# ACT copies the placed gates out ahead of the gelu of the same step, in the first part of the expert mixer

## The chip, the cores and the metric

The kernel runs on one core of one Trainium2 chip. The metric is the device time of one execution in microseconds (us); the time before is the median of three runs. Engines: PE (matrix multiply; PEld is its weight load), DVE (vector), ACT (scalar), POOL (GpSimd), SP (issues DMAs).

## The reference

One inference step of a two-layer backbone over 128 context tokens and 512 latent tokens of width 1024. Each layer is a token mixer (gated convolution with a recurrence in layer 0, attention in layer 1) and then an expert mixer, which the change touches. For the expert mixer each token has 8 heads; a head picks 16 of 128 x 128 experts by the sums of two score tables, and an expert is one row of `u_tab` and one row of `v_tab`:

```python
sc, pos = lax.top_k(cand, PEER_TOPK)
eidx = jnp.take_along_axis(cidx, pos, axis=-1)
gate = jax.nn.softmax(sc, axis=-1)
a = jax.nn.gelu(jnp.einsum('td,tkd->tk', xi, u_tab[ei]), approximate=False)
return jnp.einsum('tk,tkd->td', gi * a, v_tab[ei])
```

All is float32.

## The kernel before

The expert mixer is `peer`, called once per layer. It treats the five blocks of 128 tokens in two ways. Two blocks are *gathered*: POOL fetches each token's expert rows by indirect DMA, DVE multiplies a fetched row with the token (`meet`, L1610) and later adds a weighted row of `v` (`add_row`, L1628). The three others are *dense*: the products of all 384 tokens with all 16384 experts are computed, and the gates, which are zero but for 128 experts of a token, are laid out as a dense table in DRAM.

The dense blocks take two parts. The first has `STEPS` = 128 steps, one per tile of 128 experts. In step i

- DVE turns a tile of `u` (`turn`, L1601; it runs two steps ahead, with two buffers `u_turned` between it and PE),
- PE multiplies it with the tokens (`dots_of`, L1370, 8 products in 16 instructions) into one of four PSUM banks,
- ACT takes the gelu out of that bank (`gelu`, L1446) and sends it to DRAM (`store_acts`, L1451; two buffers `act_out`, so gelu i waits for the landing of store i - 2).

Beside this the dense gates are built. A group is 8 tokens; there are 16 groups in each of the stages 1, 2 and 3 of 32 steps (stage 0 is spent on choosing experts), in 26 steps of stages 1 and 2 and in 20 steps of stage 3 (`groups_at`). A group n passes through four engines' programs in successive steps:

1. step i, DVE: `one_hot(n)` writes two tables of ones and zeros (L1590, L1592);
2. step i + 1, ACT: `apply_gate(n)` scales one of them by the gates (L1465, 8 instructions);
3. step i + 2, PE: `place_gates(n)`, right behind that step's dots, multiplies the two tables (L1387, two halves of 8 instructions) into PSUM banks 6 and 7; half 0 waits until ACT has copied out half 0 of group n - 1, half 1 for half 1, and the whole for `apply_gate(n)`;
4. step i + 3, ACT: `gates_out(n)` copies both halves to `arena` (L1475, two instructions), and for an odd n sends 1 MB to DRAM (L1480, semaphore `gates_stored`).

The order on each engine is the order in which its block is written; engines meet only at semaphores. ACT's block is a loop over steps; in a step it takes the gelu, its store, at the start of a stage a softmax (`softmax`, L1440) and `choice_out` (L1458), then `gates_out`, `apply_gate`, and at the end `activate` (L1486, the gelu of eight gathered products). PE's block in a step is `dots_of`, `turn_choice` (L1377), `place_gates`. In the first three steps of stages 1 to 3 DVE also runs `decode` (L1549 to L1573), and in stages 0 to 2 it chooses experts for a later block (`choose`, L1521 to L1537), its first part in one step, its second in the next, none in the third. Both kinds of stores (L1451, L1480) are issued by ACT, on one queue; SP issues the loads of `u` (L1253).

The second part (L1417, L1628, L1635) multiplies the gated products with `v`; it isn't changed.

Of the kernel before, what the change touches and what calls it, by code (L numbers as in the profile page):

```python
# [1105 lines left out]
def groups_at(i):  # L1106

    stage, r = divmod(i, STAGE)
    first, steps = 16 * (stage - 1), 20 if stage == 3 else 26
    if i < 0 or not 1 <= stage <= 3 or not 5 <= r < 5 + steps:  # L1110
        return range(0)
    return range(first + 16 * (r - 5) // steps, first + 16 * (r - 4) // steps)
# [8 lines left out]
def decode_at(i):  # L1121

    stage, r = divmod(i, STAGE)
    return (stage - 1, r) if 1 <= stage <= 3 and r < 3 else None
# [26 lines left out]
def halves_by(i):  # L1151

    return range(picks_by(i - 1) // 8, picks_by(i) // 8)


def peer(nc, s, m, a, l):
# [88 lines left out]
    with phase(nc, f"q_full q_out s_full s_out keys_full keys_out w_landed*2 late_landed*2 u_landed*{U_SLOTS} u_ready dots_full "  # L1245
# [176 lines left out]
        @block.scalar  # L1422
        def _(act):
            def query_out(c, late):
                at = c + CHUNKS * late
                act.wait_ge(S.q_full, at + 1)
                if at >= 2:
                    act.wait_ge(S.s_full, at - 1)
                n = ND if late else N0
                nc.scalar.activation(q_cur[:, c % 2, 0:n], m.ps[:, c % 2, 0:n], ACT.Copy).then_inc(S.q_out, 1)  # L1430

            def scores_out(c, late):
                act.wait_ge(S.s_full, c + CHUNKS * late + 1)
                t0, t1 = (GATHERED, T) if late else (0, GATHERED)
                src = m.ps[:, 2 + c % 2, 0:(t1 - t0) * P].rearrange("p (t n) -> p t n", n=P)
                nc.scalar.activation(scores[:, t0:t1, c // 2, c % 2], src, ACT.Copy).then_inc(S.s_out, 1)

            def softmax(t):
                act.wait_ge(S.soft_ready, t + 1)
                nc.scalar.activation(gate, gate, ACT.Exp).then_inc(S.exp_ready, 1)  # L1440

            def gelu(i):
                act.wait_ge(S.dots_full, i + 1)
                if i >= ACT_SLOTS:
                    act.wait_ge(S.act_stored[i % ACT_SLOTS], 16 * (i // ACT_SLOTS))
                nc.scalar.activation(act_out[:, i % ACT_SLOTS], m.ps[:, i % 4, 0:ND], ACT.Gelu)\  # L1446
                    .then_inc(S.gelu_done, 1)

            def store_acts(i):
                act.wait_ge(S.gelu_done, i + 1)  # L1450
                act.dma_start(m.act_rows[i, :, 0:ND], act_out[:, i % ACT_SLOTS])\  # L1451
                    .then_inc(S.act_stored[i % ACT_SLOTS], 16)

            def choice_out(t):
                act.wait_ge(S.choice_full, t + 1)
                if t >= 1:
                    act.wait_ge(S.hot_ready, GROUPS * t)
                nc.scalar.activation(chosen, m.ps[:, 4, 0:3 * P].rearrange("p (s t) -> p s t", s=3), ACT.Copy)\  # L1458
                    .then_inc(S.choice_out, 1)

            def apply_gate(n):
                act.wait_ge(S.hot_ready, n + 1)
                for tok in range(HOT):
                    one, at = hot_i[:, n % 2, tok], n % GROUPS * HOT + tok
                    e = nc.scalar.activation(one, one, ACT.Copy, scale=chosen[:, 2, at:at + 1])  # L1465
                e.then_inc(S.gated, 1)

            def gates_out(n):
                g = n // 2
                for half in range(2):  # L1470
                    act.wait_ge(S.gates_full, 2 * n + half + 1)
                    if n % 2 == 0 and half == 0 and g >= 2:
                        act.wait_ge(S.gates_stored[g % 2], 16 * (g // 2))
                    at = n % 2 * HOT + half * 4
                    nc.scalar.activation(gates[:, g % 2, :, at:at + 4].rearrange("p i t -> p t i"),  # L1475
                                         m.ps[:, 6 + half, :].rearrange("p (t i) -> p t i", t=4), ACT.Copy)\
                        .then_inc(S.gates_out, 1)
                if n % 2 == 1:
                    act.wait_ge(S.gates_out, 2 * n + 2)
                    act.dma_start(m.gate_rows[g], gates[:, g % 2]).then_inc(S.gates_stored[g % 2], 16)  # L1480

            def activate(half):
                act.wait_ge(S.dotted, 8 * half + 8)
                if half >= 2:
                    act.wait_ge(S.weight_ready, half - 1)
                nc.scalar.activation(active[:, half % 2], dots[:, half % 2], ACT.Gelu).then_inc(S.gelu_ready, 1)  # L1486

            for g in range(4):
                act.wait_ge(S.keys_full, g + 1)
                nc.scalar.activation(keysT[:, 4 * g:4 * g + 4], m.ps[:, 4 + g, :].rearrange("p (c n) -> p c n", n=P),  # L1490
                                     ACT.Copy).then_inc(S.keys_out, 1)
            for at in range(2 * CHUNKS):
                query_out(at % CHUNKS, at // CHUNKS)
                if at >= 1:
                    scores_out((at - 1) % CHUNKS, (at - 1) // CHUNKS)
                if at == CHUNKS + 4:
                    softmax(0)
            scores_out(CHUNKS - 1, 1)
            softmax(1)
            for i in range(LAST):  # L1500
                if i < STEPS:
                    gelu(i)
                    store_acts(i)
                    if decode_at(i) is not None and decode_at(i)[1] == 0:
                        softmax(GATHERED + decode_at(i)[0])
                    if decode_at(i - 3) is not None and decode_at(i - 3)[1] == 2:
                        choice_out(decode_at(i - 3)[0])
                    for n in groups_at(i - 3):
                        gates_out(n)
                    for n in groups_at(i - 1):  # L1510
                        apply_gate(n)
                for half in halves_by(i - 1):
                    activate(half)
# [690 lines left out]
```

## Time and profile before

| what | value |
|---|---|
| time, median of 3 runs | 5009.06 us (5006.87 to 5018.08) |
| the profiled execution | 5015.78 us, of which the span of its instructions is 5014.0 us |
| PE busy | 4407.7 us (88%) |
| DVE busy | 3067.9 us (61%) |
| ACT busy | 916.6 us (18%) |
| POOL busy | 1383.8 us (28%) |
| first part of the mixer, gelu of step 0 to gelu of step 127 | layer 0: 1019 to 1905 us; layer 1: 3374 to 4266 us |
| granted TensorE clock, mean | 0.940 |

Busy time counts an engine's own instructions; DMA issues and waits on semaphores are not in it. "Idle before" is an engine's gap ahead of an instruction, put down to the semaphore that came last. The granted clock is the share of full speed (2.4 GHz) that TensorE was given, 0.5 being its lower level.

### The profile page before, as it was taken

How to read it: one execution, taken by the hardware profiler on the slowest of the kernel's cores; microseconds unless marked ns; L12 is line 12 of the kernel's file. 1: busy time of each engine (PE TensorE's matmuls, PEld its weight loads, DVE VectorE, ACT ScalarE, POOL GpSimd, SP SyncE). 2: the span in 40 equal slices, each digit the busy share in tenths (PEclk: the TensorE clock that was granted, in tenths of full speed). 3: DMA queues.
4: the chain of work that ended last, by engine and by line, in shares of the span. 5: the costliest groups of instructions: out<-in, count | busy, mean ns of one | idle time of the engine just before them, and what ended most of it. 6: DMA issues, size and time to landing. Idle time of an engine off the chain costs nothing. (4 is left out here: it accounts for less than half of the span.)

```text
span 5014.0 us, 44244 instructions
## 1 busy us (share of the span) xinstructions
PE 4407.7 (88%) x14942; PEld 2478.5 (49%) x14942; DVE 3067.9 (61%) x5509; ACT 916.6 (18%) x1966; POOL 1383.8 (28%) x1300
## 2 busy tenths in 40 slices
PE   7997677988999889999998799789899988999997
PEld 3545655644555554444443444655455555444443
DVE  2003753888888765565551543588887776655565
ACT  1002211101434340000001242210143434000000
POOL 0002620233111224554430331023211122444552
PEclk9998888999999999999998799899999999999998
DMA  4117016589777889999972400659977788999996
GB/s 159 67 42 207 4 38 139 140 255 284 213 222 216 263 263 376 384 391 384 391 277 80 126 1 17 139 165 291 260 220 221 213 260 272 392 388 390 387 392 230
DMA packets 639152, 1147.92 MB, mean 229 GB/s; under 512 B 53540, under 2 KB 425380, under 8 KB 632648
## 3 DMA queue, kind: packets, MB, share of 16 engines
q1 hardware_dynamic: 445040, 507.40, 33.6%
q0 software_dynamic: 148032, 537.01, 31.0%
q10 hardware_dynamic: 45856, 100.69, 5.4%
q8 instruction: 120, 1.97, 0.2%
q14 instruction: 104, 0.85, 0.1%
HBM read 1040.78 MB, written 104.14 MB: 228 GB/s over the span
## 5 line engine op out<-in xcount | busy, mean ns | idle before, releaser
L1370 PE MATMUL ps<-hT,arena 128*128 128x384 f32 x4096 | 1387.3, 498 | 101.0 <-DVE arena L1601 100.7
L1370 PEld LDWEIGHTS ps<-hT,arena 128*128 128x128 f32 x4096 | 790.2, 196 | 648.0 <-DVE arena L1601 93.2
L1310 POOL DMA_INDIRECT arena<-in_peer_v,small x512 | 549.2, 1073 | 1583.9 <-DVE mod_shift L1628 1475.4
L1306 POOL DMA_INDIRECT arena<-in_peer_u,small x512 | 579.0, 1131 | 835.1 <-DVE tail L1610 490.0
L1417 PE MATMUL ps<-arena 128*128 128x512 f32 x1536 | 696.6, 615 | 82.6 <-DMA arena<-in_peer_v 82.6
L1417 PE MATMUL ps<-arena,mod_scale 128*128 128x512 f32 x1536 | 664.4, 593 | 0.0
L1628 DVE SCALAR_TENSOR_TENSOR mod_shift<-arena,tail,mod_shift 128x1024 f32<-128x1024 f32 x508 | 651.7, 1283 | 12.2 <-DVE h L1573 1.0
L1610 DVE CUSTOM_DVE_ANT_0 arena<-arena,h 128x1024 f32<-128x1024 f32 x512 | 617.0, 1214 | 15.2 <-DMA arena<-in_peer_u,small 12.2
L1417 PEld LDWEIGHTS ps<-arena 128*128 128x128 f32 x1536 | 301.5, 198 | 476.1 <-issue 474.4
L1601 DVE STREAM_TRANSPOSE arena<-arena 128x1024 f32<-128x1024 f32 x256 | 317.9, 1242 | 301.2 <-PE ps L1370 277.4
L1417 PEld LDWEIGHTS ps<-arena,mod_scale 128*128 128x128 f32 x1536 | 292.5, 190 | 366.7 <-issue 366.0
L1635 DVE TENSOR_TENSOR arena<-arena 128x384 f32<-128x384 f32 x128 | 71.2, 557 | 535.9 <-DMA arena<-act_rows 535.9
L1387 PE MATMUL ps<-arena,mod_scale 128*128 128x128 f32 x1536 | 227.2, 310 | 126.1 <-ACT arena L1475 109.5
L1446 ACT ACTIVATE arena<-ps 128x384 f32<-128x384 f32 x256 | 124.9, 488 | 1143.1 <-PE ps L1370 1141.8
L1349 PE MATMUL ps<-hT,arena 128*128 128x256 f32 (+1 forms) x1024 | 294.1, 442 | 12.6 <-DMA arena<-in_peer_w_q 12.6
L1387 PEld LDWEIGHTS ps<-arena,mod_scale 128*128 128x128 f32 x1536 | 208.8, 218 | 181.5 <-issue 137.6
L1486 ACT ACTIVATE tail<-tail 128x8 f32<-128x8 f32 x64 | 13.3, 207 | 1327.3 <-DVE tail L1610 1324.7
L1465 ACT ACTIVATE arena<-arena,h 128x128 f32<-128x128 f32 x768 | 234.0, 389 | 29.4 <-ACT arena L1446 15.3
L1349 PEld LDWEIGHTS ps<-hT,arena 128*128 128x128 f32 x1024 | 196.0, 196 | 86.0 <-DMA arena<-in_peer_w_q 13.2
L542 PE MATMUL ps<-hT,arena 128*128 128x512 f32 x384 | 198.1, 598 | 2.2 <-PEq L70 2.2
L1475 ACT ACTIVATE arena<-ps 128x512 f32<-128x512 f32 x192 | 186.7, 1076 | 39.3 <-ACT arena L1446 39.3
L251 PE MATMUL ps<-hT,silu_c 128*2 128x128 f32 x1152 | 137.2, 281 | 44.8 <-DMA hT<-in_w_mod 44.8
(270 smaller groups left out, 3937.1 us busy)
## 6 DMA issues: line engine op xcount, KB each, us to landing
arena<-in_peer_u SPq DMA_DIRECT2D x1024, 128.0 KB, 5.0
arena<-in_peer_v SPq DMA_DIRECT2D x128, 1024.0 KB, 12.5
act_rows<-arena ACTq DMA_DIRECT2D x256, 192.0 KB, 4.2
gate_rows<-arena ACTq DMA_DIRECT2D x48, 1024.0 KB, 7.2
arena<-gate_rows SPq DMA_DIRECT2D x32, 1536.0 KB, 40.6
hT<-in_w_mod SPq DMA_DIRECT2D x144, 256.0 KB, 3.7
arena<-in_peer_w_q SPq DMA_DIRECT2D x64, 512.0 KB, 15.0
arena<-act_rows SPq DMA_DIRECT2D x32, 768.0 KB, 19.6
```

Source lines behind the costliest of these rows:

```text
L542: pe.matmul(m.ps[:, b, :], lhsT, m.hT[:, k, 0:512], start=first, stop=end)
L1306: pool.indirect_dma_start(u_rows[:, p % U_ROWS], None, u_table, at).then_inc(m.u_landed[p % U_ROWS], 16)
L1310: pool.indirect_dma_start(v_rows[:, p % V_ROWS], None, v_table, at).then_inc(m.v_landed[p % V_ROWS], 16)
L1349: mm = pe.matmul(m.ps[:, c % 2, 0:end - first], w[:, k, c % 4 * P:(c % 4 + 1) * P], m.hT[:, k, first:end], start=(k == 0), stop=(k == KD - 1))
L1370: mm = pe.matmul(m.ps[:, i % 4, 0:ND], u_turned[:, i % 2, k], m.hT[:, k, N0:N], start=(k == 0), stop=(k == KD - 1))
L1387: mm = pe.matmul(m.ps[:, 6 + half, c * P:(c + 1) * P], hot_j[:, n % 2, tok], hot_i[:, n % 2, tok], start=True, stop=True)
L1417: mm = pe.matmul(m.ps[:, o, :], w_in[k // ABLOCK % 2][:, k % ABLOCK, t * P:(t + 1) * P], v_in[v % V_SLOTS][:, k % VBLOCK, half * 512:(half ...
L1465: e = nc.scalar.activation(one, one, ACT.Copy, scale=chosen[:, 2, at:at + 1])
L1475: nc.scalar.activation(gates[:, g % 2, :, at:at + 4].rearrange("p i t -> p t i"), m.ps[:, 6 + half, :].rearrange("p (t i) -> p t i", t=4), ...
L1601: dve.transpose(u_turned[:, i % 2].rearrange("p c (m a) -> p m c a", m=4), u_raw[:, i % U_SLOTS].rearrange("p m (c b) -> p m c b", b=32)). ...
L1610: dve.tensor_tensor_reduce(row, row, m.h[:, p // P], 1.0, 0.0, ALU.mult, ALU.add, dots[:, half % 2, j:j + 1]).then_inc(S.dotted, 1)
L1628: dve.scalar_tensor_tensor(y, row, by, y, ALU.mult, ALU.add).then_inc(S.dve_added, 1)
```

## The change

In ACT's loop over steps the two lines of `gates_out` move from behind the gelu, its store, the softmax and `choice_out` to the head of the step. Nothing else moves; the orders of PE, DVE, POOL and SP stay as they are.

```diff
             for i in range(LAST):
                 if i < STEPS:
+                    for n in groups_at(i - 3):
+                        gates_out(n)
                     gelu(i)
                     store_acts(i)
                     if decode_at(i) is not None and decode_at(i)[1] == 0:
                         softmax(GATHERED + decode_at(i)[0])
                     if decode_at(i - 3) is not None and decode_at(i - 3)[1] == 2:
                         choice_out(decode_at(i - 3)[0])
-                    for n in groups_at(i - 3):
-                        gates_out(n)
                     for n in groups_at(i - 1):
                         apply_gate(n)
```

ACT before, two steps in the third stage of layer 0 (steps 64 to 95), in each of which a group is copied out; `dots_full` is raised by PE at the end of a step's dots, `gates_full` by each half of a placement, `hot_ready` by DVE's `one_hot`:

```order
L1446 ACTIVATE arena<-ps 128x384 [waits act_stored1,dots_full]
L1451 DMA act_rows<-arena 128x384 [waits gelu_done]
L1475 ACTIVATE arena<-ps 128x4x128 [waits gates_stored1,gates_full]
L1475 ACTIVATE arena<-ps 128x4x128 [waits gates_full]
L1446 ACTIVATE arena<-ps 128x384 [waits act_stored0,dots_full]
L1451 DMA act_rows<-arena 128x384 [waits gelu_done]
L1475 ACTIVATE arena<-ps 128x4x128 [waits gates_full] x2
L1480 DMA gate_rows<-arena 128x2048 [waits gates_out]
L1465 ACTIVATE arena<-arena,h 128x128 [waits hot_ready]
L1465 ACTIVATE arena<-arena,h 128x128 x7
```

The same two steps with the change:

```order
L1475 ACTIVATE arena<-ps 128x4x128 [waits gates_stored1,gates_full]
L1475 ACTIVATE arena<-ps 128x4x128 [waits gates_full]
L1446 ACTIVATE arena<-ps 128x384 [waits act_stored1,dots_full]
L1451 DMA act_rows<-arena 128x384 [waits gelu_done]
L1475 ACTIVATE arena<-ps 128x4x128 [waits gates_full] x2
L1480 DMA gate_rows<-arena 128x2048 [waits gates_out]
L1446 ACTIVATE arena<-ps 128x384 [waits act_stored0,dots_full]
L1451 DMA act_rows<-arena 128x384 [waits gelu_done]
L1465 ACTIVATE arena<-arena,h 128x128 [waits hot_ready]
L1465 ACTIVATE arena<-arena,h 128x128 x7
```

The copies now stand ahead of the wait for `dots_full`; the 1 MB store stands directly ahead of a gelu and its store, and `apply_gate` directly behind them.

ACT before, at the start of the third stage (step 64), where a softmax stands in the step:

```order
L1446 ACTIVATE arena<-ps 128x384 [waits act_stored0,dots_full]
L1451 DMA act_rows<-arena 128x384 [waits gelu_done]
L1440 ACT_TABLE_LOAD
L1440 ACTIVATE h<-h 128x128 [waits soft_ready]
L1475 ACTIVATE arena<-ps 128x4x128 [waits gates_stored1,gates_full]
L1475 ACTIVATE arena<-ps 128x4x128 [waits gates_full]
L1486 ACT_TABLE_LOAD [waits weight_ready]
```

The same step with the change:

```order
L1475 ACTIVATE arena<-ps 128x4x128 [waits gates_stored1,gates_full]
L1475 ACTIVATE arena<-ps 128x4x128 [waits gates_full]
L1446 ACTIVATE arena<-ps 128x384 [waits act_stored0,dots_full]
L1451 DMA act_rows<-arena 128x384 [waits gelu_done]
L1440 ACT_TABLE_LOAD
L1440 ACTIVATE h<-h 128x128 [waits soft_ready]
L1486 ACT_TABLE_LOAD [waits weight_ready]
```

Here the copies pass the softmax and its table load too.

## Rows read from the trace of the kernel before

**Rows 1.** The page, busy tenths of PE and the transfer rate, in 40 slices.

```profile
PE   7997677988999889999998799789899988999997
GB/s 159 67 42 207 4 38 139 140 255 284 213 222 216 263 263 376 384 391 384 391 277 80 126 1 17 139 165 291 260 220 221 213 260 272 392 388 390 387 392 230
```

**Rows 2.** The page, groups of instructions by line: busy us, mean ns, idle before.

```profile
L1370 PE MATMUL ps<-hT,arena 128*128 128x384 f32 x4096 | 1387.3, 498 | 101.0 <-DVE arena L1601 100.7
L1387 PE MATMUL ps<-arena,mod_scale 128*128 128x128 f32 x1536 | 227.2, 310 | 126.1 <-ACT arena L1475 109.5
```

**Rows 3.** Who waited for whom, whole run: us in total, times, longest.

```profile
PE ps L1387 <- ACT arena L1475: 109.5, 48, 3.6
```

**Rows 4.** Line L1465 (apply_gate), who waited for it: us, times.

```profile
  PE ps L1387: 16.4, 26
```

**Rows 5.** Timeline of PE, layer 0, stage 3: start us, us, what, idle before.

```profile
1742.36 3.42 PE L1387 MATMUL ps<-arena,mod_scale 128*128 128x128 f32 x16 [2.19 <-ACT arena L1475]
1756.97 2.05 PE L1387 MATMUL ps<-arena,mod_scale 128*128 128x128 f32 x16 [0.63 <-ACT arena L1465]
```

**Rows 6.** Timeline of ACT, the same stretch.

```profile
1751.22 0.49 ACT L1446 ACTIVATE arena<-ps 128x384 f32<-128x384 f32 x1 [8.12 <-PE ps L1370]
...
1752.12 1.96 ACT L1475 ACTIVATE arena<-ps 128x512 f32<-128x512 f32 x2 [0.40 <-ACT arena L1446]
...
1754.47 2.45 ACT L1465 ACTIVATE arena<-arena,h 128x128 f32<-128x128 f32 x8 [0.40 <-ACT arena L1475]
1756.83 0.47 ACT L1446 ACTIVATE arena<-ps 128x384 f32<-128x384 f32 x1
...
1757.70 2.45 ACT L1465 ACTIVATE arena<-arena,h 128x128 f32<-128x128 f32 x8 [0.40 <-ACT arena L1446]
```

**Rows 7.** Timeline of ACT, steps without a wait of PE: the starts of gelu.

```profile
1394.34 0.49 ACT L1446 ACTIVATE arena<-ps 128x384 f32<-128x384 f32 x1
1401.55 0.49 ACT L1446 ACTIVATE arena<-ps 128x384 f32<-128x384 f32 x1 [6.72 <-PE ps L1370]
1702.64 0.49 ACT L1446 ACTIVATE arena<-ps 128x384 f32<-128x384 f32 x1 [3.72 <-PE ps L1370]
1707.80 0.49 ACT L1446 ACTIVATE arena<-ps 128x384 f32<-128x384 f32 x1 [4.67 <-PE ps L1370]
```

**Rows 8.** Stretches A:B: length; PE, PEld, DVE, ACT, POOL busy (count); clock; DMA share; GB/s.

```profile
1260.28:1429.53 169.25, 155.43 (x608) 98.92 (x606) 134.93 (x268) 74.16 (x173) 23.37 (x25) 0.98 0.75 219
1707.80:1884.20 176.40, 148.57 (x577) 100.46 (x576) 115.14 (x123) 77.08 (x182) 50.54 (x48) 0.92 0.88 272
sum 1028.54, PE 917.38 PEld 595.08 DVE 770.29 ACT 450.84 POOL 193.60; mean PE 152.90 PEld 99.18 DVE 128.38 ACT 75.14 POOL 32.27
```

**Rows 9.** Timeline of PE and of DVE at the start of stages 2 and 3.

```profile
1440.49 3.76 PE L1387 MATMUL ps<-arena,mod_scale 128*128 128x128 f32 x16 [3.60 <-ACT arena L1475]
...
1450.33 1.25 DVE L1601 STREAM_TRANSPOSE arena<-arena 128x1024 f32<-128x1024 f32 x1 [1.42 <-PE ps L1370]
...
1672.04 1.25 DVE L1601 STREAM_TRANSPOSE arena<-arena 128x1024 f32<-128x1024 f32 x1 [0.44 <-PE ps L1370]
```

**Rows 10.** Who waited for whom, 1260 to 1430 us.

```profile
DVE arena L1601 <- PE ps L1370: 29.9, 11, 4.7
```

**Rows 11.** Who waited for whom, 1713 to 1889 us.

```profile
DVE arena L1601 <- PE ps L1370: 44.2, 13, 7.4
DVE mod_scale L1590 <- PE ps L1387: 16.2, 7, 4.4
```

**Rows 12.** Timeline of DVE, one step of stage 1 with a group and a choice.

```profile
1319.50 1.25 DVE L1601 STREAM_TRANSPOSE arena<-arena 128x1024 f32<-128x1024 f32 x1 [1.83 <-PE ps L1370]
...
1326.70 1.28 DVE L1628 SCALAR_TENSOR_TENSOR mod_shift<-arena,tail,mod_shift 128x1024 f32<-128x1024 f32 x1
```

**Rows 13.** Line L1451 (store of a gelu), whole run.

```profile
DMA to landing us min/median/max: 1.8/4.2/9.2
```

**Rows 14.** Line L1480 (store of gates), whole run.

```profile
DMA to landing us min/median/max: 3.9/7.2/12.5
```

## The prediction

> **What bounds the kernel now.** I read the page first: PE is the busiest engine, in the slices of the mixer's first part (9 to 14 and 27 to 33 of 40) at 7 to 9 tenths [rows 1]. Then its groups: dots and placements. A placement, 16 instructions, stands idle 126.1 us in all before its 96 runs, 109.5 of it for `gates_out` on ACT [rows 2]. The table of waits gives the count: 48 waits, the longest 3.6 us [rows 3]; 26 more, 16.4 us, are for `apply_gate` [rows 4]. The timeline shows why. PE ends the dots of a step and wants to place group n into the banks that hold group n - 1. ACT has waited idle through those dots (8.12 us before the gelu) although group n - 1 lay finished in PSUM all that time, then takes gelu and store, and only 0.90 us after the gelu's start begins the copy (1751.22 to 1752.12) [rows 6]. So PE waits 2.19 us [rows 5]. In a step that follows such a copy, `apply_gate` ends late, 5.70 us after the gelu's start (1754.47 + 2.45 against 1751.22), and PE waits 0.63 us for that [rows 5, 6].
>
> A step without any wait is 5.16 us from gelu to gelu, and 7.21 us with a placement (1394.34 to 1401.55) [rows 7]: the placement costs its own 2.05 us [rows 5].
>
> **What goes: term A.** I take six stretches, one for each stage 1, 2 and 3 of both layers, that hold the placements but those at stage starts. Four are like the first row of rows 8: 24 steps with 14 placements, which without waits would be 24 x 5.16 + 14 x 2.05 = 152.5 us. Two are like the second: 20 steps with 16 placements, 20 x 5.16 + 16 x 2.05 = 136.0 us. Together 882 us; they took 1028.5 us [rows 8]. The excess is 146 us, 16.7 in the first row and 40.4 in the second. It is made of waits and of what follows them: of the 125.9 us of waits [rows 3, 4] 4 x 3.6 = 14.4 belong to stage starts, 111.5 remain, and the other 35 us is half clock: after a wait of 2.19 us the placement took 3.42 us for 2.05 [rows 5], and the granted clock is 0.92 over the stage 3 stretch, 0.98 over the other [rows 8].
>
> With the change the copy (1.96 us for both halves [rows 6]) runs inside the dots of the step, which take 5.16 us, and its data are there: PE placed the group before it began those dots. The cover for it is thus PE's own work, of an engine that has to run anyway. `apply_gate` moves up by the length of the copy: where no copy stands before it, it ends 3.32 us after the gelu's start (1757.70 + 2.45 against 1756.83 [rows 6]), while PE's next placement begins 5.16 us or more after; 1.84 us to spare. ACT's whole step becomes 3.32 + 1.96 + 0.33 for the 1 MB store's issue (the time of the other issue that ACT makes), some 5.6 us of 7.21, so ACT is no bound. The gelu waits for a copy only if that copy waits for PE, and the placement stands ahead of the dots in PE's order, so it can't. I take all of term A: **-146 us**.
>
> **Term B, the stage starts.** At step 64 and 96 the copy passes the softmax and its table load too, and the 3.60 us wait goes [rows 9]. But there DVE decodes, and it has almost no idle time: it waited 1.42 us and 0.44 us for PE before its next turn [rows 9]. PE arrives earlier and then waits for DVE. Bounds: 0, and 4 starts x (3.60 + 1.7 of half clock, the placement being 3.76 us for 2.05) = 21 us. I take what DVE has idle: **-2 us**.
>
> **Term C, DVE is late next.** In 1260 to 1430 us DVE waits 29.9 us for PE [rows 10], so it has some 139 us of work for a stretch that is to shrink from 169.3 to 152.5. It holds on the mean, with 13 us to spare; not in every step. A step with one-hots and the first part of a choice takes 1319.50 to 1326.70, 7.2 us, and a row of 1.28 us more [rows 12], 8.5 us against PE's 5.16 or 7.21. It is late by 1.3 to 3.3 us; the two turned buffers cover 5.16 - 1.25 = 3.9 us, and a second heavy step behind it may use that up. In stage 3 DVE waits 44.2 us for dots and 16.2 us for placements [rows 11], so it has 116 us of work for 136. Bounds: 0, and the whole gain of stages 1 and 2, 4 x 16.7 = 67 us. I take 3 us per stretch of stages 1 and 2, nearer the low end since the mean leaves room: **+12 us**.
>
> **Term D, the stores on ACT's queue.** The 1 MB store moves from 4 or more us ahead of the next gelu's store to about 1 us ahead of it. It lands 7.2 us after issue in the median, 12.5 at most [rows 14]; the gelu's own store needs 4.2 in the median, 1.8 at least [rows 13]. No row shows the two this close. Bounds: if they don't hinder each other, 4.2 us; if the small one is served last, 7.2 + 1.8 = 9.0 us in the median and 12.5 + 1.8 = 14.3 us at worst after the large one's issue. The gelu that waits for it comes two steps later, 10.3 us, and 1.84 us may pass then before PE feels it: some 12.4 us. So the median is hidden, and the worst costs 1.9 us; if a quarter of the 48 do that, 23 us. Stage 3 will also ask for more per us (272 GB/s x 176/136 = 352 [rows 8], while the second part runs at 384 to 392 [rows 1]). I take 8: **+8 us**, between 0 and 23.
>
> The Trainium skill (DMA: Bandwidth & Descriptors, "Queues, rings and completion order") states that ACT's queue is one ring on each DMA engine and that its descriptors are consumed in ring order: a rule against this order of stores. By it the late end of term D would hold and the sum would be -113; by the median row alone term D is nothing and the sum is -136.
>
> **Sum:** -146 - 2 + 12 + 8 = -128 us. The profiled execution took 5015.78 us and would take 4888; the median of the runs is 6.7 us lower, 5009.06, and becomes 4881 us.
>
> **The rivals.**
>
> 1. *Another engine holds a part.* If DVE's bursts line up badly, stages 1 and 2 give nearly all of their 67 us back, 55 more than term C counts: 4881 + 55 = 4936. If instead transfers bind in stage 3, whose DMA engines are busy 0.88 of 176.4 us [rows 8], that stretch can't fall below 155: 19 us less gain in each layer, 4881 + 38 = 4919. For it: DVE busy 135 of the 152.5 us to come [rows 8]. Against it: the rate in the second part is 1.4 times that of this stretch [rows 1, 8].
> 2. *The wait changes its name.* ACT's step ends with `activate`, which waits for DVE's products; a late DVE then holds up the next copy, which now stands right behind it, and PE waits for the copy as before. If half of term A survives, 5009 - 73 = 4936; if three quarters do, 4972. Against it: ACT has 1.6 us to spare in a step with a placement.
> 3. *Slower: the small store behind the large one.* If under the denser traffic the 1 MB store takes 14.4 us, twice its median, the gelu's store lands at 16.2 us, 3.8 past the 12.4 that are free; with the whole of ACT's step, copies included, stuck behind a gelu and its clock loss of 1.7 us on PE each time, 48 x (3.8 + 1.7) = 264 us against 148 gained: 5009 + 116 = 5125; it decides from a landing of about 12 us in the median. Against it: the maximum now is 12.5 [rows 14]. By the ring order that the Trainium skill states on the same page this would be the mechanism; by the rows its size is not reached.
>
> **How the numbers follow.** Forecast 0.72, own range 4855 (all of A and some more of B) to 4905 (C and D at twice their sizes). Rival 1 0.17, rival 2 0.06, rival 3 0.04, and 0.01 that nothing can be seen. 0.2% is 10 us, which is about what runs of this kernel differ by (5006.87 to 5018.08), so it is what a measurement can tell from no change. Faster 0.94, same 0.02, slower 0.04. The range runs from 4855 to 4936, over most of rival 1.
>
> **What would show it.** In the new profile the wait of L1387 for L1475 should be gone or under 15 us, that for L1465 too; the mean of a placement's instruction clearly below its 310 ns [rows 2]; the stretches at 153 to 157 and 136 to 142 us; their clock near 1; DVE's waits for dots much smaller and PE's wait for L1601 a little larger than 101 us, at stage starts. If the placements still wait for ACT, or a gelu waits for a DMA of `act_rows`, rival 2 or 3 is at work; if PE's wait for L1601 grows by 50 us, rival 1.

## The result, and the profile after

The changed kernel takes 4846.5 us (median of 4 runs, 4843.3 to 4848.9) against 5008.6 us (4 runs), a ratio of 0.967 with a 95% interval of 0.9658 to 0.9681: 162 us less, where the forecast was 128 less. 4846.5 lies below the low end of the range, 4855. The profiled execution's span is 4847.0 us, 167.0 us less than that of before.

PE's groups after (busy us, mean ns | idle before, and who ended it), to be read against [rows 2]:

```profile
L1370 PE MATMUL ps<-hT,arena 128*128 128x384 f32 x4096 | 1377.8, 495 | 121.1 <-DVE arena L1601 120.6
L1387 PE MATMUL ps<-arena,mod_scale 128*128 128x128 f32 x1536 | 187.0, 275 | 0.0
```

The 126.1 us of idle time before placements are gone to the last tenth, and the placements themselves take 187.0 us instead of 227.2: none runs at half clock any more. PE's wait for DVE's turns grew by 20 us.

The six stretches of the prediction, cut at the same steps (A:B, length, busy time of PE, PEld, DVE, ACT and POOL, granted clock, DMA share, GB/s), against [rows 8]:

```profile
1257.03:1405.89 148.86, 148.86 (x610) 97.99 (x609) 134.35 (x267) 75.25 (x174) 22.94 (x25) 1.00 0.89 254
...
1666.30:1798.09 131.79, 131.79 (x577) 89.40 (x576) 113.97 (x123) 79.14 (x184) 56.88 (x47) 1.00 1.04 340
...
sum 858.99, PE 858.99 PEld 570.75 DVE 765.39 ACT 459.27 POOL 204.80; mean PE 143.16 PEld 95.12 DVE 127.56 ACT 76.55 POOL 34.13
```

PE is busy in every microsecond of them (148.86 of 148.86) at full clock. 1028.5 us became 859.0: 169.5 less, and 23 us less than the 882 that the prediction held to be the least possible. So something in that floor was wrong. The eight steps or so at each start of stages 2 and 3 (four stretches, steps 63 to 71 and 95 to 103), of before and then of after:

```profile
sum 219.74, PE 195.21 PEld 122.11 DVE 180.30 ACT 54.74 POOL 42.02; mean PE 48.80 PEld 30.53 DVE 45.08 ACT 13.68 POOL 10.51
```

```profile
sum 222.90, PE 193.47 PEld 117.15 DVE 181.57 ACT 54.16 POOL 43.14; mean PE 48.37 PEld 29.29 DVE 45.39 ACT 13.54 POOL 10.78
```

They gave nothing: 3 us more here, 1.2 us more in the other profiled execution of the changed kernel (221.0). PE's waits in the first of them (steps 63 to 71 of layer 0), two rows of before and one of after, show why:

```profile
PE ps L1387 <- ACT arena L1475: 3.6, 1, 3.6
PE ps L1370 <- DVE arena L1601: 1.6, 1, 1.6
```

```profile
PE ps L1370 <- DVE arena L1601: 6.2, 2, 5.1
```

The wait for ACT is gone and the wait for DVE's turns has grown by as much and more. Over the four starts PE's idle time after is 29.4 us (222.90 less 193.47), all of it waits for the turns; before, 9.6 us were. All else together differs by 0.6 us.

ACT after, in a stretch of stage 1, against [rows 6]:

```profile
1274.30 0.49 ACT L1446 ACTIVATE arena<-ps 128x384 f32<-128x384 f32 x1 [1.82 <-PE ps L1370]
1274.82 0.33 ACTq L1451 DMA_DIRECT2D act_rows<-arena  x1
1275.19 2.44 ACT L1465 ACTIVATE arena<-arena,h 128x128 f32<-128x128 f32 x8 [0.41 <-ACT arena L1446]
1277.55 1.88 ACT L1475 ACTIVATE arena<-ps 128x512 f32<-128x512 f32 x2
1279.45 0.33 ACTq L1480 DMA_DIRECT2D gate_rows<-arena  x1
1281.25 0.49 ACT L1446 ACTIVATE arena<-ps 128x384 f32<-128x384 f32 x1 [1.82 <-PE ps L1370]
```

`apply_gate` ends 3.33 us after the gelu's start, the copies follow at once, and ACT then waits 1.82 us for the dots. The step from gelu to gelu, with a placement in it, is 1274.30 to 1281.25: 6.95 us, not 7.21.

### Where the floor was wrong

The trace of before shows what a placement costs in two ways. Its first weight load and its first product, PEld and PE, in the step of [rows 7] that the prediction took as one without a wait:

```profile
1394.30 1.86 PEld L1387 LDWEIGHTS ps<-arena,mod_scale 128*128 128x128 f32 x16 [0.61 <-ACT arena L1465]
```

```profile
1394.30 2.05 PE L1387 MATMUL ps<-arena,mod_scale 128*128 128x128 f32 x16
```

and at the first placement of stage 3, where `apply_gate` was done early and no group stood before it:

```profile
1712.44 2.08 PEld L1387 LDWEIGHTS ps<-arena,mod_scale 128*128 128x128 f32 x16
```

```profile
1712.76 1.95 PE L1387 MATMUL ps<-arena,mod_scale 128*128 128x128 f32 x16
```

In the second the weights are loaded 0.32 us before the product starts, while the dots still run; in the first the load begins with the product, because `apply_gate` ended just then, and the idle time is booked on PEld alone. That step is 6.95 us (gelu to gelu, 1712.96 to 1719.91), the first 7.21. A placement is thus worth 6.95 - 5.16 = 1.79 us, and the 2.05 of the prediction contained 0.26 us of lateness that no wait of PE shows. With 1.79 the six stretches come to 4 x (24 x 5.16 + 14 x 1.79) + 2 x (20 x 5.16 + 16 x 1.79) = 859 us, which is what was measured.

The Trainium skill (TensorE: Matmul & The Clock Gate, "Step-by-step: what each phase is for") states that weight loads, alone among PE's instructions, may run ahead of products still in flight. The 0.32 us here agree.

### The profile page after: what moved, and what is told of

Read it like the earlier page. It is cut to its first block and busy times, and to the rows that moved or that the text cites. A ratio compares the mean times of both kernels' runs of the same rounds, so it can differ in the third digit from the quotient of the medians.

```text
span 4847.0 us, 44244 instructions
## 1 busy us (share of the span) xinstructions
PE 4338.9 (90%) x14942; PEld 2440.8 (50%) x14942; DVE 3063.9 (63%) x5509; ACT 920.8 (19%) x1966; POOL 1396.0 (29%) x1300
## 5 line engine op out<-in xcount | busy, mean ns | idle before, releaser
L1370 PE MATMUL ps<-hT,arena 128*128 128x384 f32 x4096 | 1377.8, 495 | 121.1 <-DVE arena L1601 120.6
L1370 PEld LDWEIGHTS ps<-hT,arena 128*128 128x128 f32 x4096 | 780.0, 193 | 666.3 <-DVE arena L1601 115.5
L1306 POOL DMA_INDIRECT arena<-in_peer_u,small x512 | 592.0, 1156 | 796.2 <-DVE tail L1610 454.3
L1628 DVE SCALAR_TENSOR_TENSOR mod_shift<-arena,tail,mod_shift 128x1024 f32<-128x1024 f32 x508 | 651.8, 1283 | 12.1 <-DVE h L1573 1.0
L1417 PEld LDWEIGHTS ps<-arena,mod_scale 128*128 128x128 f32 x1536 | 291.8, 190 | 367.4 <-issue 366.9
L1446 ACT ACTIVATE arena<-ps 128x384 f32<-128x384 f32 x256 | 125.4, 490 | 978.2 <-PE ps L1370 978.2
L1465 ACT ACTIVATE arena<-arena,h 128x128 f32<-128x128 f32 x768 | 234.9, 388 | 38.8 <-ACT arena L1446 38.8
L1349 PEld LDWEIGHTS ps<-hT,arena 128*128 128x128 f32 x1024 | 193.7, 194 | 82.9 <-DMA arena<-in_peer_w_q 10.4
L1387 PEld LDWEIGHTS ps<-arena,mod_scale 128*128 128x128 f32 x1536 | 186.6, 192 | 25.4
L1387 PE MATMUL ps<-arena,mod_scale 128*128 128x128 f32 x1536 | 187.0, 275 | 0.0
```

Source lines behind the costliest of these rows:

```text
L1306: pool.indirect_dma_start(u_rows[:, p % U_ROWS], None, u_table, at).then_inc(m.u_landed[p % U_ROWS], 16)
L1349: mm = pe.matmul(m.ps[:, c % 2, 0:end - first], w[:, k, c % 4 * P:(c % 4 + 1) * P], m.hT[:, k, first:end], start=(k == 0), stop=(k == KD - 1))
L1370: mm = pe.matmul(m.ps[:, i % 4, 0:ND], u_turned[:, i % 2, k], m.hT[:, k, N0:N], start=(k == 0), stop=(k == KD - 1))
L1387: mm = pe.matmul(m.ps[:, 6 + half, c * P:(c + 1) * P], hot_j[:, n % 2, tok], hot_i[:, n % 2, tok], start=True, stop=True)
L1417: mm = pe.matmul(m.ps[:, o, :], w_in[k // ABLOCK % 2][:, k % ABLOCK, t * P:(t + 1) * P], v_in[v % V_SLOTS][:, k % VBLOCK, half * 512:(half ...
L1628: dve.scalar_tensor_tensor(y, row, by, y, ALU.mult, ALU.add).then_inc(S.dve_added, 1)
```

## The experiments

The theory after the result: ACT's order alone held PE in the groups; the gain is PE's waits (108.9 us within the stretches, 95.1 for the copies and 13.8 for `apply_gate`), the clock that fell after them, and 0.26 us for each placement that began late; the stage starts are DVE's. Lengths of stretches are compared in the traces, since in the changed kernel's two profiled executions they agree to 0.01 us, while stage 0 and the second part differ by some 5 us between executions of one kernel. The kernel before ran beside each set; its medians there were 5013.2, 5014.3 and 5016.7 us.

**Half of the copies ahead.** On the changed kernel:

```diff
                     for n in groups_at(i - 3):
-                        gates_out(n)
+                        gates_out(n, [0])
                     gelu(i)
                     store_acts(i)
+                    for n in groups_at(i - 3):
+                        gates_out(n, [1])
```

> Only the first of the two copies of a group stands ahead of the gelu; the second stands behind the gelu's store, as before. Theory (PE is held by the copies' place in ACT's order, and each copy's lateness adds to the wait): PE places half 0 at once and waits about 1.0 us for half 1 (the second copy ends 0.9 + 0.98 us after the gelu's start, half 0 of a placement takes 0.9) in the 44 placements that follow a placement of the step before: 44 to 57 us more than the changed kernel, 4890 to 4905 us. Rival 1 (any wait there costs the same, since the clock falls after it): near 4930. Rival 2 (it is the first copy alone that holds PE): 4847.

4908.7 us, ratio to before 0.9788 (0.9771 to 0.9805), 62 us more than the changed kernel. PE in it:

```profile
1702.72 1.05 PE L1387 MATMUL ps<-arena,mod_scale 128*128 128x128 f32 x8
1704.91 1.16 PE L1387 MATMUL ps<-arena,mod_scale 128*128 128x128 f32 x8 [1.14 <-ACT arena L1475]
```

```profile
PE ps L1387 <- ACT arena L1475: 55.0, 48, 1.4
```

Each half waits for its own copy: half 0 starts at once, half 1 after 1.14 us. The stretches grew by 7.1 (stages 1, 2) and 17 us (stage 3), 62.4 in all. 44 waits of 55.0/48 = 1.15 us are 50.4, and 44 x 0.26 = 11.4 more for a half that begins late make 61.8. The expectation took the wait at about 1.0 us and named no such start; its upper end, 4905, is 4 us short. Neither rival fits; the clock stayed at 1.00 in these stretches, so waits of this length cost no clock here.

**The copies ahead, but not at stage starts.**

```diff
-                    for n in groups_at(i - 3):
+                    late = decode_at(i) is not None
+                    for n in groups_at(i - 3) if not late else range(0):
                         gates_out(n)
                     gelu(i)
...
+                    for n in groups_at(i - 3) if late else range(0):
+                        gates_out(n)
```

> The change everywhere but in the first three steps of a stage, where the copies stand behind the softmax as before. Theory (DVE's decode sets the end of these steps, PE's wait for the copy is hidden under it): 4846 +- 4 us, the four stage starts as long as in both kernels (54 to 57 us from step 63 to 71 and 95 to 103). Rival (the waits of 3.6 us and the clock after them were a gain too): 4 x 5.3 = 21 us more, 4867 us.

4860.1 us, ratio 0.9689 (0.967 to 0.9708); its interval and that of the changed kernel overlap. The number lies between the two expectations, so the trace decides. Its four stage starts:

```profile
sum 219.19, PE 194.57 PEld 119.96 DVE 181.77 ACT 54.82 POOL 42.77; mean PE 48.64 PEld 29.99 DVE 45.44 ACT 13.71 POOL 10.69
```

```profile
PE ps L1387 <- ACT arena L1475: 14.4, 4, 3.6
```

The stage starts are not longer than in the changed kernel (222.9, and 221.0 in its other execution) although the four waits of 3.6 us are back in them, and the six stretches are the changed kernel's; the theory holds. This execution is 17 us longer than the changed kernel's all the same: some 6 us in stage 0 of layer 0 and most of the rest behind the last groups of each layer, where the two kernels do the same.

**The kernel before, with PE's waits filled.**

```diff
-            def place_gates(n):
+            def place_gates(n, fill):
+                for c in range(8 if fill else 0):
+                    pe.matmul(m.ps[:, 5, c % 4 * P:(c % 4 + 1) * P], m.ident[:], m.ident[:], start=True, stop=True)
                 pe.wait_ge(S.gated, n + 1)
...
-                    place_gates(n)
+                    place_gates(n, len(groups_at(i - 3)) > 0 and decode_at(i) is None)
```

> The kernel before, with eight products of the unit matrix with itself into an unused PSUM bank put into PE's wait wherever a placement follows one of the step before (some 1.8 us of work in a wait of 2.2 us; it adds work and changes no output). Theory (of the gain some 35 us was the clock that fell after PE's waits): the waits stay as time and the clock stays up: 4972 to 4985 us, with a granted clock near 1 in the group stretches. Rival (the clock's loss there has another cause): 5009 us or more, the clock as in the kernel before.

4976.9 us, ratio 0.9927 (0.991 to 0.9945): useless work made the kernel before 36 us faster. PE in it, and a stretch of stage 3:

```profile
1731.60 5.33 PE L1370 MATMUL ps<-hT,arena 128*128 128x384 f32 x16
1736.76 1.95 PE L1382 MATMUL ps<-ident 128*128 128x128 f32 x16
1739.12 2.02 PE L1389 MATMUL ps<-arena,mod_scale 128*128 128x128 f32 x16 [0.41 <-ACT arena L1477]
1740.98 10.49 PE L1370 MATMUL ps<-hT,arena 128*128 128x384 f32 x32
```

```profile
1706.15:1869.62 163.47, 156.87 (x769) 111.48 (x768) 115.08 (x123) 77.25 (x182) 53.92 (x48) 1.00 0.94 291
```

The placement still starts only when the copy is done, and the step is 9.38 us (1731.60 to 1740.98 between two steps' dots; the kernel before took 9.45 us, 1725.40 to 1734.85, in a step that ran at nearly full clock), so the wait is all there; but the clock is 1.00 where it was 0.92 [rows 8]. The six stretches together are 37.5 us shorter. That is the clock's share of the gain; the prediction had worked it out as 35.

**The kernel before, with `apply_gate` ahead of the gelu in place of the copies.**

```diff
                 if i < STEPS:
+                    for n in groups_at(i - 1):
+                        apply_gate(n)
                     gelu(i)
...
-                    for n in groups_at(i - 1):
-                        apply_gate(n)
```

> The kernel before, with apply_gate moved ahead of the gelu in place of the copies. Theory: PE's wait for apply_gate goes (16.4 us and the 0.26 us of a just-in-time placement some 40 times), the 48 waits for the copies stay: 4980 to 4995 us. Rival (what counts is that ACT works during the dots, whichever work it is): near 4847.

4988.0 us, ratio 0.9937 (0.9913 to 0.9961). Its placements:

```profile
L1387 PE MATMUL ps<-arena,mod_scale 128*128 128x128 f32 x1536 | 227.0, 311 | 112.8 <-ACT arena L1475 112.8
```

The waits for `apply_gate` are gone and those for the copies have stayed, clock loss included (311 ns). So the rival is out: which of ACT's work runs under the dots decides, and each piece removes only the wait that PE had for it. The six stretches are 25.5 us shorter; the expectation's terms, 16.4 us of waits and some 40 starts at 0.26, come to 27. The copies' share is the rest of the gain, by difference: no run moved the copies and left `apply_gate` late.

**ACT delayed before every `apply_gate`,** by six and by nine short copies:

```diff
             def apply_gate(n):
+                for d in range(6):
+                    nc.scalar.activation(m.tail[:, 48 + 4 * d:52 + 4 * d], m.ident[:, 0:4], ACT.Copy)
                 act.wait_ge(S.hot_ready, n + 1)
```

> The changed kernel with six short ACT copies (some 1.2 us together, to unused columns) ahead of each apply_gate. Theory (apply_gate has 1.84 us to spare before the dots end, 1.5 us before the first weight load of the placement could start): no difference, 4844 to 4852 us, group stretches of 148.9 and 131.8 us. Rival (ACT's step in groups is the next bound): some 0.5 us or more per group, 48 us and more.

> The same with nine copies, some 1.8 us, so that apply_gate ends just when the dots end in those steps whose dots follow no placement. Theory (a placement whose semaphores come just at the end of the dots costs 2.05 us instead of 1.79, as its first weight load can't run under the dots): about 0.26 to 0.4 us for some 50 of 96 groups, 13 to 20 us more, 4860 to 4866 us, with steps of 7.2 us where the changed kernel has 6.95. Rival (there is no such start-up; 7.21 us steps of the kernel before had another cause): 4847.

4852.2 and 4859.9 us, ratios 0.9675 (0.9656 to 0.9695) and 0.9691 (0.9671 to 0.971). The stretches are those of the changed kernel to 0.01 us, but for one of stage 3 that is 0.44 us longer. The copies were shorter than taken:

```profile
1674.84 0.96 ACT L1463 ACTIVATE tail<-ident 128x4 f32<-128x4 f32 x9 [0.40 <-ACT arena L1446]
1675.71 2.43 ACT L1467 ACTIVATE arena<-arena,h 128x128 f32<-128x128 f32 x8
1679.11 0.49 ACT L1446 ACTIVATE arena<-ps 128x384 f32<-128x384 f32 x1 [0.96 <-PE ps L1370]
```

With nine, `apply_gate` still ends 0.96 us before the gelu. So both show room on ACT, and neither tests the start-up; the second missed its point, and its 4859.9 us, near the 4860 of its theory, is no support for it.

**ACT delayed only where the placement follows a step without one.** Four copies of 128 columns and five or twelve short ones, under `if not groups_at(i - 2)`:

```diff
-            def apply_gate(n):
+            def apply_gate(n, late):
+                for d in range(4 if late else 0):
+                    nc.scalar.activation(m.ps[:, 5, d * P:(d + 1) * P], m.ident[:], ACT.Copy)
+                for d in range(5 if late else 0):
+                    nc.scalar.activation(m.tail[:, 48 + 4 * d:52 + 4 * d], m.ident[:, 0:4], ACT.Copy)
```

> The changed kernel with ACT kept busy for some 1.75 us (four copies into an unused PSUM bank, five short ones) ahead of those apply_gates alone whose placement follows a step without one: 9 in each stretch of stages 1 and 2, 4 in each of stage 3. apply_gate then ends about 5.1 us after the gelu's start, where the dots end after 5.16 and the first weight load could have begun after 4.84. Theory (a placement whose wait ends just at the end of the dots has lost the 0.26 us that its first weight load runs under the dots, though no wait can be seen): steps of 7.2 us instead of 6.95 there, stretches of 151.2 and 132.8 us, 11 us in all. Rival (the 2.05 us of a placement in the kernel before were something else, such as the copies of ACT beside it): stretches of 148.9 and 131.8 us.

> The same with some 2.5 us of work, so that apply_gate ends about 5.8 us after the gelu's start, 0.65 us after the dots' end. Theory: 0.65 + 0.26 us per such placement, stretches of 157 and 135.4 us, some 40 us in all, with waits of PE for L1465 that can be seen. Rival (no start-up): 0.65 us each, stretches of 154.7 and 134.4 us.

With five, 4853.4 us, ratio 0.9677 (0.9659 to 0.9695), and the changed kernel's stretches: again too short, `apply_gate` ended before the weight load could begin. With twelve, 4871.1 us, ratio 0.9713 (0.9695 to 0.9731), and it came late:

```profile
1274.34 2.05 PE L1387 MATMUL ps<-arena,mod_scale 128*128 128x128 f32 x16 [0.21 <-ACT arena L1469]
```

```profile
PE ps L1387 <- ACT arena L1469: 10.4, 48, 0.5
```

```profile
1256.42:1409.58 153.16, 151.23 (x608) 96.86 (x606) 134.35 (x267) 93.56 (x333) 23.00 (x25) 1.00 0.88 246
1675.08:1808.77 133.69, 132.86 (x577) 89.06 (x576) 114.62 (x123) 86.43 (x248) 57.61 (x48) 1.00 1.05 342
```

The wait that can be seen is 0.22 us each (10.4/48). The stretch of stage 1 is 4.3 us longer for 9 such placements, that of stage 3 1.9 us for 4: 0.48 us each. So 0.26 us of each is the start-up, at full clock. Sized for a wait of 0.65 us, it was 0.2, and the totals missed; by the wait that came about, the rival without a start-up would give 2 us for the stretch of stage 1, not 4.3.

**More work on DVE in each step.**

```diff
                     turn(i + 2)
+                    c(dve.tensor_copy(m.tail[:, 48:96], m.ident[:, 0:48]))
+                    c(dve.tensor_copy(m.tail[:, 48:96], m.ident[:, 0:48]))
```

> The changed kernel with two short copies more on DVE in each step of the first part (some 0.4 us a step, to unused columns). Theory (in the group stretches DVE has room and its bursts are covered by the two turned buffers, at stage 0 and the stage starts it sets the pace): stretches stay at 148.9 and 131.8 us within 1 us, the other steps lengthen by about 0.4 us each, some 20 us a layer: 4880 to 4890 us. Rival (term C of the prediction: DVE's bursts are about to bind): the four stretches of stages 1 and 2 lengthen too, by 3 to 9 us each.

4900.1 us, ratio 0.9771 (0.9751 to 0.979). The two copies are 0.15 and 0.19 us. The stretches:

```profile
1276.48:1428.34 151.86, 150.29 (x610) 97.75 (x609) 144.01 (x316) 74.67 (x173) 23.36 (x24) 1.00 0.86 247
1692.83:1828.12 135.29, 132.48 (x577) 89.25 (x576) 121.48 (x165) 78.17 (x183) 46.62 (x46) 1.00 1.03 328
```

They grew by 3.0 and 3.5 us, the low end of the rival: 24 x 0.34 = 8 us of work were mostly, not wholly, covered. DVE's bursts cost nothing in the changed kernel, and begin to with a third of a microsecond more per step. They reach PE in part by way of ACT:

```profile
1412.43 2.45 ACT L1465 ACTIVATE arena<-arena,h 128x128 f32<-128x128 f32 x8 [4.30 <-DVE arena L1592]
1414.78 1.93 ACT L1475 ACTIVATE arena<-ps 128x512 f32<-128x512 f32 x2
1415.96 2.02 PE L1387 MATMUL ps<-arena,mod_scale 128*128 128x128 f32 x16 [0.89 <-ACT arena L1475]
```

`apply_gate` waits 4.30 us for DVE's one-hots, the copies stand behind it in ACT's order, and PE waits for the copies again. It is rival 2 of the prediction, the wait that changes its name, through `apply_gate` and not through `activate`; in the changed kernel `apply_gate` never waits for DVE.

**The gathered rows paced away from the stage starts,** less and more:

```diff
-        return 48 + 16 * (stage - 1) + (r + 1) // 2
+        return 48 + 16 * (stage - 1) + max(0, r - 4) * 16 // 27
...
-        return 80 + 9 * (r + 1) // 8
+        return 80 + (6 * (r + 1) // 8 if r < 8 else 6 + 30 * (r - 7) // 24)
```

The second has `max(0, r - 7) * 16 // 24` and `(r + 1) // 2 if r < 8 else 4 + 32 * (r - 7) // 24`. The changed kernel ran beside it once more.

> The changed kernel with the gathered rows of stages 1 to 3 paced away from the stage starts: in stages 1 and 2 their 16 picks are spread over steps 5 to 31 of a stage, in stage 3 6 picks in the first eight steps and 30 in the other 24. Theory (DVE sets the stage starts and has room in the group stretches): 2 picks less (2 x 2.5 us) at each start of stages 1 and 2 and 3 less at stage 3, some 17 us a layer, the stretches unchanged: 4810 to 4820 us. Rival (the stretches have no room for it): what is saved at the starts comes back in the stretches, 4840 to 4850.

> The changed kernel once more, on the same chip as the next run and in as many rounds. All theories: 0.967 of the kernel before, near 4850 us.

> The changed kernel with the gathered rows paced further away from the stage starts: in stages 1 and 2 none in the first eight steps and 16 in the other 24, in stage 3 4 and 32. Theory (DVE sets the stage starts, and has some 0.2 us a step of room in the stretches): each stage start 5 to 10 us shorter than in the changed kernel, the stretches within 2 us of 148.9 and 131.8, 20 to 40 us in all against the changed kernel of the same job. Rival (the stretches have no room, or transfers take it back in the second part): the same time as the changed kernel.

4849.6 us, ratio 0.9674 (0.9658 to 0.969); the changed kernel again 4851.3, 0.9669 (0.9656 to 0.9683); the second pace 4860.1, 0.9688 (0.9675 to 0.9702). Neither is faster than the changed kernel. The starts of stages 2 and 3 shrank by 1.6 to 3.2 us each in the first, not by 5 to 7, with unchanged stretches, and the total doesn't show it. In the second, time came back in stage 3, in the stretch and in the four steps behind it:

```profile
1666.16:1801.79 135.63, 132.77 (x577) 89.22 (x576) 118.39 (x130) 78.72 (x184) 60.05 (x49) 1.00 0.99 326
```

131.8 became 135.6 and 134.3 us in the two layers. In the first of them, PE waits 2.2 us for a turn and DVE's turns wait 9.6 us for loads of `u`; in the four steps behind it these are 3.7 and 8.8 us. So late loads have a part in it, beside DVE's own work. That relieved steps shrink at all fits DVE as what holds them; why they shrink by less than the work that was taken away is left open.

## Why the prediction was wrong in its size

- **What bounds the kernel, and what the change removes:** right. Both waits of PE vanished with the change of ACT's order alone; `apply_gate` moved by itself took its own wait away and left that for the copies.
- **Term A, -146 us: the step that failed.** The text said "A step without any wait is 5.16 us from gelu to gelu, and 7.21 us with a placement". The 7.21 us step held a hidden 0.26 us, and a placement was taken at 2.05 us for 1.79, which put the floor of the six stretches at 882 us for 859. Measured: -169.5 us, made of 108.9 us of waits, 37.5 us of clock (the filled kernel) and 0.26 us for the 82 placements that began late (88 less the first of each stretch), 21 us; together 168. The text's 111.5 us of waits took off only the copies' 14.4 us at stage starts; `apply_gate`'s 2.6 us there belong off too, and the clock's share is then 37.6 us by its own sum. The trace of before had the right step in six places, the first placement of each stage, the one of stage 3 at 1712.96 to 1719.91.
- **Term B, -2 us:** right in kind; the stage starts belong to DVE and gave nothing (+3 us in one execution, +1 in the other). PE's wait for the turns took over, 100.7 to 120.6 us over the run. The -2 adds up DVE's two waits of layer 0 alone.
- **Term C, +12 us:** measured 0. PE never waited for DVE in the stretches. The run with more work on DVE shows that the cover was nearly used up, so the mechanism is there and its size was taken too high.
- **Term D, +8 us:** measured 0. After, the landing of a gelu's store (L1451) and of a gate store (L1480):

```profile
DMA to landing us min/median/max: 1.8/5.2/9.8
```

```profile
DMA to landing us min/median/max: 3.9/7.7/10.2
```

The small store lands 1.0 us later in the median than in [rows 13]. No gelu waits for one, since all waits of L1446 are for PE, 255 of them; the store with the least room landed 1.1 us before the gelu that reuses its buffer.

```profile
  PE ps L1370: 978.2, 255
```

The two stores also came less close than the text took: ACT waits for the dots between them, so the small one is issued 4.4 to 4.6 us behind the large one in 28 of 48 cases and 1.6 to 2.3 us behind it in 20, where the text had about 1 us. The 28 take 3.7 us to land in the median, the 20 take 6.3. In all 48 the small store lands after the large one, by 0.2 us at the least, and so it was before; the ring order that the Trainium skill states (DMA: Bandwidth & Descriptors, "Queues, rings and completion order") agrees. But it isn't what raised the median: the 48 went from 5.1 to 4.3 us, the other stores from 4.0 to 5.5. (The time that is free, 12.4 us in the text, is 10.3 + 1.84 = 12.1 by its own terms; nothing hangs on it.)

The sum was -128; with 23 us more from A, 5 us less from B and nothing given back for C and D (20) it is -166, and the span shrank by 167.0. The range's low end, 4855, allowed for C and D at nothing (4861), but not for an error in the floor of A, which passed for a bound. Rival 1 came about only at the stage starts, where it had been in the forecast. Its other half, that transfers keep a stage 3 stretch from falling below 155 us, is refuted: the stretch took 131.8 us, with a DMA share of 1.04 and 340 GB/s, so a share of 1 is no ceiling as the text took it to be. Loads of `u` do come later now: DVE's turns wait 7.8 us for them in that stretch, where none such is listed before, and none of it reached PE. Rivals 2 and 3 came about not at all in the changed kernel: ACT keeps 1.82 us to spare, and no gelu waits for a store.

## What to carry to other kernels

Look for an engine that waits for another's long piece of work while it holds back something that the other will need next, and put that ahead of the wait: here a copy of 1.96 us fitted under dots of 5.16. A floor is to be read from the fastest step of its kind in the trace, and checked against several; a step without a visible wait may still hold one, and on PE it is to be sought in the row of the weight loads. When waits of PE go, count the clock that fell after them, here a third on top of the waits.

## What the runs showed that had not been expected

- A group of products whose semaphore comes in the moment the products before it end costs 0.26 us, with no idle time on PE's own row.
- Eight useless products in PE's wait (1.95 us of 2.19) held the granted clock at 1.00 instead of 0.92 and made the kernel 0.7% faster. Waits of 1.14 us left the clock at 1.00 without any filling; waits of 2.2 us did so only in part of the steps (in the kernel before, 1731.0 to 1740.2 us ran at 1.00, 1740.2 to 1751.2 us at 0.84).
- Short ACT copies of 4 columns follow each other at 0.1 us (nine in 0.96 us), though each is listed with 0.19.
- Stretches in which PE is the bound repeat to 0.01 us from one execution of the changed kernel to another; stage 0 of layer 0 (gelu of step 0 to gelu of step 31) took 179.9 us in one and 185.2 in the other.
